# Weight sums of the last MLP: copies moved into the mixer's output stage, additions at four chosen tiles of the first tail

## Chip, cores and metric

The kernel runs on one core of a Trainium2 chip. The metric is the device time of one execution in microseconds (us). Five engines work from their own instruction queues: TensorE (PE in the profile), VectorE (DVE), ScalarE (ACT), GpSimd (POOL) and SyncE (SP), which issues most DMA transfers. The core has 16 DMA engines. Transfers that SP and ScalarE issue go through hardware queues (q1 in the profile), transfers that POOL issues through the software queue q0.

## What is computed

The reference is a transformer-like block followed by a second block of two layers, on 512 tokens of width 1024, in float32:

```
x = first_block(x, ...)        # attention + pooling + SSM mixer, w_out, top-2 of 16 experts
for i in range(2):             # second_block
    h = x * (1 + scale) + shift
    y = mla_mixer(h, ...) if i == 0 else s5_mixer(h, ...)
    x = layer_norm(ALPHA * x + (1 + gate) * y)
    h = x * (1 + scale) + shift
    y = relu(h @ w1[i] + b1[i]) ** 2 @ w2[i] + b2[i]
    x = layer_norm(ALPHA * x + (1 + gate) * y)
```

The change concerns the weights `w2[1]` (4096 x 1024), the down projection of the last MLP. The kernel multiplies it in 2 x 2 blocks in a scheme that needs seven block products in place of eight; four of them use sums of weight blocks. With 00, 01, 10 and 11 for the blocks (row block, column half), the sums are two = 00 + 01, right = 01 + 11, three = 00 + 01 + 11 and four = 00 + 01 + 11 + 10. Each is 4 MB. They depend on inputs alone, and are formed in DRAM by DMA transfers that POOL issues, long before they are read.

## The kernel before

The kernel is a list of stages, each an `nc.Block()` with one instruction stream for each engine. At a block's end every engine drains and meets a barrier of all engines, then the next stage begins (`Kernel.stage`). Within a stage engines meet through semaphores. A semaphore of a DMA transfer rises by 16 when the data have landed. Every float32 product is made of three products of rounded parts: ScalarE writes the high part of a weight tile (`high`), VectorE the low part (`low`), TensorE multiplies.

**The first place, `residual_stage` "mix_out" (L2162).** It is the product of the merged mixer with `w_out`, with residual and the sums of a layer norm. TensorE runs four weight tiles of 256 columns, all of whose weights are there by 980 us. POOL runs `router.widen` (L2293), which waits for two small router loads, and nothing after it. SP stores `mod_rows` (L2182) and loads the router weights. Then come `routing_stage` (L2405) and `experts_stage`. In routing, SP first issues two broadcasts `both_b` of 512 KB (L2443), a small row pair and six loads of 1 MB of the first expert's weights (L2348). VectorE uses `both_b` in `y_scaled` (L2626), for which TensorE's transposes wait. POOL makes constants (L2456 on) and later scatters the token rows by indirect DMA (L2477), which go through q0; SP waits for the scatters before it loads the next expert's tokens.

**The second place, `tail_stage` "tail0" (L3649).** It is the output product of the first mixer of the second block and the whole first MLP. Its loop runs over weight tiles n = 0 to 33 of 256 columns. A tile is 2 x 24 matmuls of 512 columns; `tile_done` rises by one for each of its two halves, so `tile_done` >= 12 means that n = 5 is through. SP loads tile n when `low(n - 3)` is done (L3722), 1 MB each. In the gaps VectorE forms parameters of the later S5 mixer (`beside(n)`): `input_powers` for n = 12 to 19 writes one room in SBUF, which SP stores to DRAM (`beside.store`, L4623) after the load of n = 18, 19, ... (`STORE_AT`). The next `input_powers` waits until that store has landed (L4723). VectorE's order in one round n is `square`, `low(n + 2)`, `hidden_low` or `add`, then `beside(n)`.

POOL ends `tail0` with `later.form` (L3755): eight DMA passes of 4 MB, four plain (`bypass`) and four accumulating (`add`), each issued when `tile_done` has reached 12, 18, 24, ... 54 and the pass before has landed (L3628 to L3632). The order is: 00 to two, + 01, two to three, + 11, 01 to right, + 11, three to four, + 10. The closing stage loads the sums at L4131, from 2332 us on.

Of the kernel before, what the change touches and what calls it, by code (L numbers as in the profile page):

```python
# [9 lines left out]
ALU = mybir.AluOpType  # L10
# [11 lines left out]
HT = HALF // P  # L22
# [2139 lines left out]
def residual_stage(k, name, halves, x, x_parts, alpha, gate, mod_rows, first, router):  # L2162

    ps = k.ps  # L2170
    base, N = halves.first[name], D // HALF
    norm_sems = [f"norm_{x}" for x in TokenNorm.SEMS]
    with k.stage(name, "x_high", "x_low", "x_scaled", "seventh_done", "evicted", "rows_stored", "router_loaded", "wide_ready", *norm_sems) as (block, s, sb):
        sq, sums = sb("sq", [P, 2, T]), sb("sums", [P, 2, T])
        norm = TokenNorm(k, s, "norm", 0, sq, sums[:, 0, :], sums[:, 1, :])
        rstd = ps[:, 3, :]

        @block.sync
        def _(sp):
            k.clear(sp)  # L2180
            for j in range(3):
                sp.dma_start(mod_rows[j:j + 1, :].rearrange("o (c p) -> p (o c)", p=P), k.mod[:, first + j * KD:first + (j + 1) * KD],  # L2182
                             allow_slow_non_contiguous=True).then_inc(s["rows_stored"], 16)
            router.load(sp, s["router_loaded"])
            sp.wait_ge(s["rows_stored"], 48)

        @block.gpsimd
        def _(pool):
            router.widen(pool, first, s["router_loaded"], s["wide_ready"])

        @block.tensor
        def _(pe):
            for n in range(N):
                outs = [ps[:, n * HT + f, :] for f in range(HT)]
                if n < N - 1:
                    halves.products(pe, base + n, x_parts, outs, arriving=(s["x_low"], 0) if n == 0 else None)
                else:
                    halves.product(pe, base + n, 0, x_parts, outs[0], final=False).then_inc(s["seventh_done"], 1)
                    halves.product(pe, base + n, 1, x_parts, outs[1], final=True)
                if n == 1:  # L2200
                    norm.pe_shift(pe)
            norm.pe_sums(pe)
            k.fill(pe, ps[:, 4, 0:P], 18)

        @block.scalar
        def _(act):
            def scaled(first, last):
                for c in range(first, last):
                    act.activation(k.x[:, c, :], k.x[:, c, :], ACT.Copy, scale=alpha).then_inc(s["x_scaled"], 1)

            for kk in range(KD):
                act.activation(x_parts[:, 0, kk], x[:, kk, :], ACT.Copy).then_inc(s["x_high"], 1)
            halves.high(act, base + 1)
            act.preload_act_table_set("natural_log_exp_and_others")
            scaled(0, 4)
            halves.high(act, base + 2)
            scaled(4, KD)
            halves.high(act, base + 3)
            for c in range(KD):
                norm.act_square(act, c)  # L2220
            norm.act_spread(act)
            act.wait_ge(norm.s["var_ready"], 1)
            act.activation(norm.rstd, norm.rstd, ACT.Ln, bias=k.eps_ln[:]).then_inc(norm.s["log_done"], 1)
            act.wait_ge(norm.s["log_done"], 1)
            act.activation(rstd, norm.rstd, ACT.Exp, scale=-0.5).then_inc(norm.s["root_done"], 1)

        @block.vector
        def _(dve):
            step = Steps(dve, s["evicted"])
            for kk in range(KD):  # L2230
                dve.wait_ge(s["x_high"], kk + 1)
                dve.tensor_tensor(x_parts[:, 1, kk], x[:, kk, :], x_parts[:, 0, kk].bitcast(F32), ALU.subtract).then_inc(s["x_low"], 1)
            halves.low(dve, base + 1)
            for n in range(N):
                if n + 2 < N:
                    halves.low(dve, base + n + 2)
                for c in range(n * HT, (n + 1) * HT):
                    if c == KD - 2:
                        dve.wait_ge(s["seventh_done"], 1)
                    else:  # L2240
                        dve.wait_ge(halves.half_used, base + n + 1)
                    dve.wait_ge(s["x_scaled"], c + 1)
                    step(dve.scalar_tensor_tensor(out=k.x[:, c, :], in0=ps[:, c, :], scalar=k.mod[:, gate + c:gate + c + 1], in1=k.x[:, c, :],
                                                  op0=ALU.mult, op1=ALU.add))
                    if c >= KD - 2:
                        norm.dve_shift(dve, c)
                if n < N - 1:
                    norm.dve_pair(dve, n)
            norm.dve_centre(dve, 0)
            norm.dve_centre(dve, 1)  # L2250
            norm.dve_var(dve)
            norm.dve_centre(dve, 2)
            norm.dve_centre(dve, 3)
# [1353 lines left out]
class WeightSums:  # L3607


    def __init__(self, k, name, w):  # L3610
        self.blocks = w.rearrange("(s two p) n -> two s p n", two=2, p=P)
        self.formed = k.stack.enter_context(k.nc.semaphore("sums_formed"))
        self.room = k.nc.dram_tensor(name, (K2 // 2, P, 4, STRIP), F32, kind="Internal").ap()

    def total(self, n):
# [3 lines left out]
    def block(self, odd, half):  # L3619
        return self.blocks[odd][:, :, half * STRIP:(half + 1) * STRIP]  # L3620

    def form(self, pool, products, every):

        two, three, right, four = (self.total(n) for n in range(4))
        n = 0
        for dst, first, then in ((two, self.block(0, 0), self.block(0, 1)), (three, two, self.block(1, 1)),
                                 (right, self.block(0, 1), self.block(1, 1)), (four, three, self.block(1, 0))):
            for src, op in ((first, ALU.bypass), (then, ALU.add)):  # L3628
                pool.wait_ge(products, every * (n + 2))
                pool.dma_start(dst, src, accum_op=op).then_inc(self.formed, 16)  # L3630
                n += 1
                pool.wait_ge(self.formed, 16 * n)  # L3632

    def source(self, i, q):

# [13 lines left out]
def tail_stage(k, layer, w_mix, x_parts, big, divided, ahead, beside, later):  # L3649
# [19 lines left out]
    with k.stage(name, "high_done", "low_done", "tile_done", "cols_step", "x_scaled", "evicted", "h_done", "x_high", "x_low", "x_ready",  # L3669
                 "relu_done", "squared", "hidden_high", "hidden_low", "added", "next_high", "next_low",  # L3670
                 *norm_sems, *S5Parameters.SEMS) as (block, s, sb):
        parts = divided
# [62 lines left out]
        def _(pool):  # L3735
# [16 lines left out]
            step(pool.tensor_scalar(vec[:, O_SCALE], g2, ALPHA_2, None, ALU.mult))  # L3752
            step(pool.tensor_scalar(vec[:, O_SHIFT], sh2, ALPHA_2, None, ALU.mult))
            pool.wait_ge(s["x_low"], KD)
            later.form(pool, s["tile_done"], 3 * HT)  # L3755

        @block.tensor
        def _(pe):
# [1618 lines left out]
def second_block(k, out, loads):  # L5377

    big, k.big_plain = shared(k, "big", [P, 2, K2 // 2, T])
    k.hp2, plain = shared(k, "h_parts_second", [P, 2, KD, T])  # L5380
    k.h, g = plain[:, 0], plain[:, 1]
    low_half, high_half = big[:, :, 0:KD, :], big[:, :, KD:, :]
    with ExitStack() as branch:
        sb = lambda n, shape: k.sb(n, shape, stack=branch)
        cq, ckv, k_pe = sb("cq", [P, QL // P, T]), sb("ckv", [P, T]), sb("k_pe", [ROPE, T])
        cos, sin = sb("cos", [ROPE, T]), sb("sin", [ROPE, T])
        latent_stage(k, loads, cq, ckv, k_pe, cos, sin)
        latent_attention_stage(k, cq, ckv, k_pe, cos, sin, low_half, k.ins["mla_w_o_2"][0])

    k.vec = k.sb("vec", [P, 9, KD])  # L5390
    parts, plain = shared(k, "late_parts", [P, 2, 2, KD, HALF])
    late = [plain[:, n].rearrange("p v k n -> p (v k n)") for n in range(2)]
    s5_input = S5Input(k, big)
    sums = WeightSums(k, "down_sums", k.ins["mlp_w2_2"][1])
    with ExitStack() as early:
        par = S5Parameters(k, lambda n, shape: k.sb(n, shape, stack=early))
        tail_stage(k, 0, k.ins["mla_w_o_2"][0], low_half, big, parts, s5_input, par, sums)
        u = late[0].rearrange("p (j g l c) -> p j g l c", j=S5_TILES, g=2, l=S5_HALF)
        both = 2 * S5_TILES * 2 * GC
        tab = S5Tables(k, late[1][:, both:])  # L5400
        resp = S5Responses(k, par, late[1][:, 0:both], lambda n, shape: k.sb(n, shape, stack=early))
        raw = late[1][:, 0:both].rearrange("p (k n) -> p k n", k=KD)
        s5_in_stage(k, u, s5_input, tab, resp)
        s5_stage(k, tab, par, resp, u, g, high_half, parts, raw)
    glu_stage(k, g, high_half, low_half, k.ins["ssm_w_out_2"][0], parts)
    closing_stage(k, 1, k.ins["ssm_w_out_2"][0], low_half, big, parts, sums, out)


def build(nc, ins, out):

    with ExitStack() as stack:
# [5 lines left out]
        with ExitStack() as strips:  # L5417
# [5 lines left out]
            k.mod_w = [flat[:, after + n * size:after + (n + 1) * size].rearrange("p (k n) -> p k n", k=KD // 2) for n in range(3)]  # L5423
            halves = Halves(k, stack)
            router = Router(k)
            mod_rows = nc.dram_tensor("mod_rows", (3, D), F32, kind="Internal").ap()
            with ExitStack() as mix:
                k.hp, plain = shared(k, "h_parts", [P, 2, KD, T], mix)
# [55 lines left out]
```

## Time and profile before

| | |
|---|---|
| time, median of 3 runs | 2647.94 us (2646.45 to 2650.1) |
| profiled execution, own time | 2652.91 us |
| its span | 2651.1 us, 33685 instructions |
| TensorE busy | 2476.3 us, 93% of the span |
| VectorE, ScalarE, POOL busy | 68%, 45%, 3% |
| DMA | 478.29 MB, mean 180 GB/s |
| software queue q0 | 22320 packets, 57.67 MB, 8.3% of 16 engines' span |

The profile gives for every instruction a start and a duration, the source line, the tiles written and read, and, where an engine was idle before it, what released it. A window view gives the busy time of each engine in a stretch, with the number of instructions that start in it, and the granted TensorE clock as a share of full speed. A DMA view gives for a stretch the packets and bytes of each queue, and for transfers issued in it the time from issue to landing.

### The profile page before, as it was taken

The numbers are of one execution on the slowest core, as the hardware profiler recorded it, in microseconds if no ns is written. First come the engines' busy times: TensorE is split into PE (matmuls) and PEld (weight loads), VectorE is DVE, ScalarE is ACT, GpSimd is POOL, SyncE is SP. The second block draws the span as 40 slices with busy tenths as digits, with TensorE's granted clock in tenths as the row PEclk, the third lists the DMA queues.
The fourth block names the chain that finished last, engine by engine and source line by source line (L and its number), as shares of the span: only waits on it lengthen the run. The fifth ranks groups of instructions, "written<-read, shape, count | busy, mean of one in ns | idle before, by whom it ended". The sixth has DMA issues, their size and how long they took to land. (4 is left out here: it accounts for less than half of the span.)

```text
span 2651.1 us, 33685 instructions
## 1 busy us (share of the span) xinstructions
PE 2476.3 (93%) x13175; PEld 1970.2 (74%) x13175; DVE 1789.7 (68%) x2553; ACT 1184.2 (45%) x1668; POOL 87.7 (3%) x184
## 2 busy tenths in 40 slices
PE   7999899999999999899988899998999989999996
PEld 5666678777777878788875457887888977788885
DVE  4899545587775666899965565675766574665557
ACT  5444422255564225588853343621324244365443
POOL 0000000000000000100001000000000000000001
PEclk9999999999999988999999999999999899999998
DMA  7887727333235744999962213598861414243446
GB/s 264 263 286 268 249 83 282 85 104 95 80 104 178 259 73 159 346 419 420 417 267 92 67 37 104 144 241 239 241 175 48 154 28 143 64 159 121 134 157 168
DMA packets 312398, 478.29 MB, mean 180 GB/s; under 512 B 29195, under 2 KB 198654, under 8 KB 302385
## 3 DMA queue, kind: packets, MB, share of 16 engines
q1 hardware_dynamic: 285392, 409.29, 45.4%
q0 software_dynamic: 22320, 57.67, 8.3%
q10 hardware_dynamic: 4528, 9.18, 0.9%
q8 instruction: 105, 1.72, 0.3%
q14 instruction: 53, 0.43, 0.1%
HBM read 431.82 MB, written 74.69 MB: 191 GB/s over the span
## 5 line engine op out<-in xcount | busy, mean ns | idle before, releaser
L2380 DVE TENSOR_TENSOR expert_parts<-w,expert_parts 128x2048 fp32r<-128x2048 f32 x102 | 232.6, 2288 | 21.2 <-ACT expert_parts L2376 20.8
L1345 PE MATMUL banks<-h_parts,ssm_parts 128*128 128x512 f32 x960 | 230.2, 397 | 0.8 <-DVE ssm_parts L1612 0.4
L3761 PE MATMUL banks<-big,late_parts 128*128 128x512 f32 x960 | 222.6, 394 | 5.7 <-DVE late_parts L3914 5.7
L2376 ACT ACTIVATE expert_parts<-w 128x2048 fp32r<-128x2048 f32 x102 | 194.7, 1916 | 60.2 <-PE banks L2387 51.8
L3761 PEld LDWEIGHTS banks<-big,late_parts 128*128 128x128 f32 x960 | 182.2, 190 | 45.2 <-issue 4.9
L1345 PEld LDWEIGHTS banks<-h_parts,ssm_parts 128*128 128x128 f32 x960 | 179.5, 189 | 43.7 <-issue 6.7
L2387 PE MATMUL banks<-expert_parts,expert_xt 128*128 128x512 f32 x816 | 192.1, 395 | 4.0 <-DVE expert_xt L2368 4.0
L2387 PEld LDWEIGHTS banks<-expert_parts,expert_xt 128*128 128x128 f32 x816 | 153.5, 190 | 36.4 <-DVE expert_xt L2368 4.7
L3761 PE MATMUL banks<-h_parts_second,late_parts 128*128 128x512 f32 x720 | 167.5, 393 | 7.5 <-DVE late_parts L3914 5.1
L3761 PEld LDWEIGHTS banks<-h_parts_second,late_parts 128*128 128x128 f32 x720 | 136.7, 190 | 36.6 <-issue 8.0
L4176 PE MATMUL banks<-h_parts_second,late_parts 128*128 128x512 f32 x512 | 159.4, 393 | 2.4 <-DVE h_parts_second L4406 2.4
L4194 PE MATMUL banks<-late_parts,big 128*128 128x512 f32 x448 | 137.9, 389 | 0.0
L882 PE MATMUL banks<-h_parts,front_parts 128*128 128x512 f32 x552 | 137.9, 400 | 0.0
L4396 DVE TENSOR_TENSOR w_parts<-w_second,late_parts 128x2048 fp32r<-128x2048 f32 x47 | 107.6, 2289 | 42.5 <-ACT late_parts L4282 42.2
L552 PE MATMUL banks<-h_parts,front_parts 128*128 128x512 f32 x576 | 132.3, 391 | 2.7 <-PEq L151 2.7
L552 PEld LDWEIGHTS banks<-h_parts,front_parts 128*128 128x128 f32 x576 | 108.0, 188 | 26.4 <-issue 4.2
L3823 ACT ACTIVATE late_parts<-w_second 128x2048 fp32r<-128x2048 f32 x35 | 66.9, 1914 | 135.2 <-PE banks L3761 135.2
L3914 DVE TENSOR_TENSOR late_parts<-w_second,late_parts 128x2048 fp32r<-128x2048 f32 x35 | 80.1, 2292 | 69.7 <-ACT late_parts L3823 68.9
L4282 ACT ACTIVATE late_parts<-w_second 128x2048 fp32r<-128x2048 f32 x47 | 89.7, 1912 | 82.2 <-DMA w_second<-in_mlp_w_dram 56.2
L552 PE MATMUL banks<-h_parts,ssm_parts 128*128 128x512 f32 x480 | 111.5, 394 | 5.9 <-DVE h_parts L1966 3.1
L882 PEld LDWEIGHTS banks<-h_parts,front_parts 128*128 128x128 f32 x552 | 101.7, 190 | 19.8
L1135 DVE SCALAR_TENSOR_TENSOR attention_mod_sum<-w,silu_c,attention_mod_sum 128x512 f32<-128x512 f32 x147 | 110.4, 751 | 4.7 <-DMA w<-in_mod_ffn_w_dram 0.3
(791 smaller groups left out, 4729.6 us busy)
## 6 DMA issues: line engine op xcount, KB each, us to landing
w_second<-in_mlp_w_dram SPq DMA_DIRECT2D x60, 1024.0 KB, 5.4
w<-in_w_exp_gate_dram SPq DMA_DIRECT2D x34, 1024.0 KB, 9.3
w<-in_w_exp_up_dram SPq DMA_DIRECT2D x34, 1024.0 KB, 9.0
w<-in_w_exp_down_dram SPq DMA_DIRECT2D x34, 1024.0 KB, 9.0
w<-in_w_in_dram SPq DMA_DIRECT2D x64, 512.0 KB, 4.6
w<-in_mod_mix_w_dram SPq DMA_DIRECT2D x24, 1024.0 KB, 5.1
down_sums<-in_mlp_w_dram POOLq DMA_DIRECT2D x6, 4096.0 KB, 31.3
w<-in_mod_ffn_w_dram SPq DMA_DIRECT2D x23, 1024.0 KB, 6.1
```

The costliest lines, as they stand in the source:

```text
L552: mm = pe.matmul(out, self.parts[:, n % 2, w, kk, f * P:(f + 1) * P], x[:, v, kk, :], start=(start and kk == 0 and j == 0), stop=(stop and ...
L882: mm = pe.matmul(ps[:, bank, :], parts[:, j, w, kk, :], k.hp[:, x, kk, :], start=(kk == 0 and n == 0), stop=(kk == KD - 1 and n == 2))
L1135: ins = dve.scalar_tensor_tensor(out=acc, in0=w, scalar=by, in1=acc, op0=ALU.mult, op1=ALU.add)
L1345: mm = pe.matmul(ps[:, t % 2, :], parts[:, t % SPLITS, w, kk, :], k.hp[:, x, kk, :], start=(kk == 0 and j == 0), stop=(kk == KD - 1 and j ...
L2376: act.activation(self.high_part(h), self.raw(h), ACT.Copy).then_inc(self.high_done, 1)
L2380: dve.tensor_tensor(self.low_part(h), self.raw(h), self.high_part(h).bitcast(F32), ALU.subtract).then_inc(self.low_done, 1)
L2387: mm = pe.matmul(out, x[:, v, first + kk, :], self.tile(h, w, kk), start=(start and kk == 0 and j == 0), stop=(stop and kk == KE - 1 and j ...
L3761: mm = pe.matmul(ps[:, bank(n, f), :], w_part(n, w)[:, kk, f * P:(f + 1) * P], x[:, v, kk, :], start=(first_chunk(n) and kk == 0 and j == ...
L4176: mm = pe.matmul(ps[:, bank(n, f), :], w_part(n, w)[:, kk, f * P:(f + 1) * P], x[:, v, kk, :], start=(kk == 0 and j == 0), stop=(kk == KD ...
L4194: mm = pe.matmul(ps[:, BANK[q] + j, :], hidden(STATIONARY[q], v)[:, kt, j * P:(j + 1) * P], strip_part(n, w)[:, kt, :], start=(kt == 0 and ...
L4282: act.activation(w_part(n, 0), raw_half(k, n), ACT.Copy).then_inc(s["high_done"], 1)
L4396: dve.tensor_tensor(w_part(n, 1), raw_half(k, n), w_part(n, 0).bitcast(F32), ALU.subtract).then_inc(s["low_done"], 1)
```

## The change

A new method `WeightSums.copy` starts four plain copies, of blocks 00, 00, 01 and 10, into the places of two, three, right and four. POOL calls it in stage `mix_out` after `widen`, and doesn't wait for the copies there. `form` in `tail0` keeps only accumulating passes, now four: two += 01 at `tile_done` 12, right += 11 at 20, three += right at 28, four += three at 54, each after the one before has landed. Before them POOL waits once for the copies (a new semaphore `sums_copied`). The object `k.sums` is made earlier in `build`, in place of in `second_block`.

```
@@ residual_stage
         def _(pool):
             router.widen(pool, first, s["router_loaded"], s["wide_ready"])
+            k.sums.copy(pool)
@@ class WeightSums
-    def form(self, pool, products, every):
+    def copy(self, pool):
+
+        for n, (odd, half) in enumerate(((0, 0), (0, 0), (0, 1), (1, 0))):
+            pool.dma_start(self.total(n), self.block(odd, half)).then_inc(self.copied, 16)
+
+    def form(self, pool, products):
 
         two, three, right, four = (self.total(n) for n in range(4))
-        n = 0
-        for dst, first, then in ((two, self.block(0, 0), self.block(0, 1)), (three, two, self.block(1, 1)),
-                                 (right, self.block(0, 1), self.block(1, 1)), (four, three, self.block(1, 0))):
-            for src, op in ((first, ALU.bypass), (then, ALU.add)):
-                pool.wait_ge(products, every * (n + 2))
-                pool.dma_start(dst, src, accum_op=op).then_inc(self.formed, 16)
-                n += 1
-                pool.wait_ge(self.formed, 16 * n)
+        pool.wait_ge(self.copied, 64)
+        for n, (dst, src, behind) in enumerate(((two, self.block(0, 1), 12), (right, self.block(1, 1), 20), (three, right, 28), (four, three, 54))):
+            pool.wait_ge(products, behind)
+            pool.dma_start(dst, src, accum_op=ALU.add).then_inc(self.formed, 16)
+            pool.wait_ge(self.formed, 16 * (n + 1))
@@ tail_stage
             pool.wait_ge(s["x_low"], KD)
-            later.form(pool, s["tile_done"], 3 * HT)
+            later.form(pool, s["tile_done"])
```

## Rows read from the trace of the kernel before

**Rows 1.** The page, part 1: busy time of TensorE, instructions.
```profile
PE 2476.3 (93%) x13175; PEld 1970.2 (74%) x13175; DVE 1789.7 (68%) x2553; ACT 1184.2 (45%) x1668; POOL 87.7 (3%) x184
```

**Rows 2.** Windows: stretch, length, busy (instructions) of five engines, clock, DMA share, GB/s.
```profile
980.00:1000.00 20.00, 20.00 (x88) 16.19 (x87) 12.99 (x18) 4.99 (x7) 0.14 (x1) 1.00 0.00 1
...
1020.00:1030.00 10.00, 8.53 (x47) 8.11 (x48) 4.06 (x9) 9.17 (x18) 0.00 (x0) 0.63 1.02 412
```

**Rows 3.** In order of time: start, duration, engine, line; end of mix_out, routing.
```profile
979.02 1.12 POOL L2301 TENSOR_TENSOR router_wide<-router_wide,mod 128x128 f32<-128x128 f32 x2 [21.04 <-DMA router_b<-in_b_router_dram]
...
1014.05 0.60 ACT L2225 ACTIVATE banks<-mix_out_sums 128x512 f32<-128x512 f32 x1
...
1015.85 0.10 POOL L2456 MEMSET routing_pair<- 128x4 f32 x1 [35.70 <-POOLq L151]
...
1024.14 0.69 DVE L2626 TENSOR_TENSOR expert_parts_plain<-expert_parts_plain,routing_both_b 128x512 f32<-128x512 f32 x1 [0.73 <-ACT expert_parts_plain L2564]
...
1055.44 1.17 POOL L2477 DMA_INDIRECT expert_rows<-expert_parts_plain,slots  x1 [38.24 <-DVE slots L2714]
```

**Rows 4.** DMA issues of the span: count, KB each, median us to landing.
```profile
down_sums<-in_mlp_w_dram POOLq DMA_DIRECT2D x6, 4096.0 KB, 31.3
...
down_sums<-down_sums POOLq DMA_DIRECT2D x2, 4096.0 KB, 20.2
...
routing_both_b<-mod_rows SPq DMA_DIRECT2D x2, 512.0 KB, 5.3
```

**Rows 5.** DMA queue, 1684 to 1694 us, first plain pass: packets, MB, share.
```profile
q0 software_dynamic: 745, 3.05, 100.9%
```

**Rows 6.** DMA queues, 409 to 411, then 423 to 425 us, POOL's zeroing.
```profile
q0 software_dynamic: 206, 0.84, 102.4%
...
q0 software_dynamic: 164, 0.67, 81.5%
q1 hardware_dynamic: 161, 0.16, 23.1%
```

**Rows 7.** In order of time, VectorE in tail0: the waits for a store.
```profile
1806.84 0.42 DVE L4856 TENSOR_TENSOR s_room<-s_held,s_b 128x256 f32<-128x256 f32 x1 [11.54 <-DMA s_inputs<-s_room]
...
1835.33 0.43 DVE L4856 TENSOR_TENSOR s_room<-s_held,s_b 128x256 f32<-128x256 f32 x1 [10.60 <-DMA s_inputs<-s_room]
```

**Rows 8.** In order of time, TensorE in tail0: its gaps.
```profile
1814.91 23.39 PE L3761 MATMUL banks<-big,late_parts 128*128 128x512 f32 x96 [3.51 <-DVE late_parts L3914]
1843.40 89.74 PE L3761 MATMUL banks<-h_parts_second,late_parts 128*128 128x512 f32 x384 [5.10 <-DVE late_parts L3914]
```

**Rows 9.** In order of time, POOL in tail0: four of eight passes.
```profile
1681.55 1.14 POOL L3630 DMA_DIRECT2D down_sums<-in_mlp_w_dram  x1 [82.03 <-PE banks L3761]
...
1779.34 1.85 POOL L3630 DMA_DIRECT2D down_sums<-in_mlp_w_dram  x1 [31.59 <-PE banks L3761]
1812.89 1.04 POOL L3630 DMA_DIRECT2D down_sums<-in_mlp_w_dram  x1 [31.70 <-DMA down_sums<-in_mlp_w_dram]
...
1922.97 1.83 POOL L3630 DMA_DIRECT2D down_sums<-in_mlp_w_dram  x1 [31.52 <-PE banks L3761]
```

**Rows 10.** In order of time, SP's DMA issues in tail0.
```profile
1772.25 0.37 SPq L3722 DMA_DIRECT2D w_second<-in_mlp_w_dram  x1
1779.02 0.37 SPq L4623 DMA_DIRECT2D s_inputs<-s_room  x1
1783.13 0.37 SPq L3722 DMA_DIRECT2D w_second<-in_mlp_w_dram  x1
1788.58 0.37 SPq L4623 DMA_DIRECT2D s_inputs<-s_room  x1
```

**Rows 11.** DMA issues, 1785 to 1790 us: us to landing.
```profile
s_inputs<-s_room SPq DMA_DIRECT2D x1, 512.0 KB, 18.2
```

**Rows 12.** Windows, TensorE alone: stretch, length, busy (matmuls), clock, DMA share, GB/s.
```profile
1820.00:1825.00 5.00, 5.00 (x24) 1.00 0.95 297
...
1843.40:1848.00 4.60, 4.60 (x11) 0.50 0.75 226
```

More of the change, by code:

```diff
@@ L3611, in __init__ @@
         self.blocks = w.rearrange("(s two p) n -> two s p n", two=2, p=P)
-        self.formed = k.stack.enter_context(k.nc.semaphore("sums_formed"))
+        self.copied, self.formed = (k.stack.enter_context(k.nc.semaphore(x)) for x in ("sums_copied", "sums_formed"))
         self.room = k.nc.dram_tensor(name, (K2 // 2, P, 4, STRIP), F32, kind="Internal").ap()
@@ L5393, in second_block @@
     s5_input = S5Input(k, big)
-    sums = WeightSums(k, "down_sums", k.ins["mlp_w2_2"][1])
     with ExitStack() as early:
         par = S5Parameters(k, lambda n, shape: k.sb(n, shape, stack=early))
-        tail_stage(k, 0, k.ins["mla_w_o_2"][0], low_half, big, parts, s5_input, par, sums)
+        tail_stage(k, 0, k.ins["mla_w_o_2"][0], low_half, big, parts, s5_input, par, k.sums)
         u = late[0].rearrange("p (j g l c) -> p j g l c", j=S5_TILES, g=2, l=S5_HALF)
@@ L5405, in second_block @@
     glu_stage(k, g, high_half, low_half, k.ins["ssm_w_out_2"][0], parts)
-    closing_stage(k, 1, k.ins["ssm_w_out_2"][0], low_half, big, parts, sums, out)
+    closing_stage(k, 1, k.ins["ssm_w_out_2"][0], low_half, big, parts, k.sums, out)
 def build(nc, ins, out):
@@ L5425, in build @@
             router = Router(k)
+            k.sums = WeightSums(k, "down_sums", k.ins["mlp_w2_2"][1])
             mod_rows = nc.dram_tensor("mod_rows", (3, D), F32, kind="Internal").ap()
```

## Prediction, made before the changed kernel was run

> **What bounds the kernel now.** I read the page first. TensorE is busy for 93% of the span [rows 1], so a microsecond counts only if TensorE loses or gains it, or if all engines wait together. The change touches two places; the windows, the order in time and the DMA view of both decide. The first place is the end of stage `mix_out`, where the copies go. TensorE runs there without a gap at a granted clock of 1.00, and the DMA engines move nothing from 980 to 1000 [rows 2]. POOL finishes `widen` at 980.1, ScalarE's last work of the stage ends at 1014.65, and routing starts on POOL at 1015.85 [rows 3]. The second place is `tail0`, where the eight passes run now. There the reader should look for DMA transfers that make a compute engine wait. VectorE waits twice for a store of S5 parameters, 11.54 and 10.60 us [rows 7], and each wait is followed by a gap on TensorE, 3.51 and 5.10 us [rows 8].
>
> **What the stores wait for.** `input_powers` may write its room again only when the store before it has landed. The store issued at 1788.58 came 9.2 us after the addition of 1779.34 [rows 9, 10] and took 18.2 us to land [rows 11]. That store blocked VectorE until 1806.8. The next load of MLP weights was queued on SP, but VectorE's order is what starves TensorE: its `low` of the coming tile stands behind `input_powers`. The second wait falls inside the plain copy of 1812.89.
>
> **Removed from the tail: four plain passes.** Additions stay at product tiles 12, 20, 28 and 54, one at a time. Tiles 12 and 30 are at 1681.55 and 1779.34 [rows 9], so a tile takes 97.8 / 18 = 5.43 us, and the four additions start at 1681.6, 1725.0, 1768.5 and again 1923.0. From row 4 an accumulating or mixed pass takes about 31 us, which the wait for `formed` hides. So the third addition ends near 1801, and none runs between there and 1923. The second stall then has no cause: **gain 5.10 us**. Its granted clock comes back too. In the 4.6 us after that gap the clock was 0.50 and 11 matmuls started, against 24 in an undisturbed 5 us [rows 12]. At 10.86 / 48 = 0.226 us each, 20 fit there, so 9 x 0.226 = **2.1 us** more. Together 7.2 us.
>
> The first stall I keep. The third addition now starts 10.9 us, exactly one weight tile, earlier. The load of 1772.25 is then 3.8 us into it and the store of 1779.02 is 10.6 us into it [rows 10], as the load of 1783.1 and the store of 1788.58 are now (3.8 and 9.2 us). Everything moves one weight tile forward: the store lands 27.4 us into the addition, at 1795.9, TensorE runs out at 1800.5 in place of 1811.4, and the gap is 3.5 us again. Bounds for this term: 0 (both stalls shift away, 5 us more gain) and 3 us worse, if the store waits for the whole 31 us. I take no change, since the phases agree to 1.4 us. Nothing else in the tail waits for these passes, and the closing stage first reads them 400 us later.
>
> **Added: four copies on POOL in `mix_out`.** POOL has nothing else there, each issue costs it 1 to 2 us [rows 9], and SP's and ScalarE's queues get nothing new. The data are 4 x 4 MB. Alone on the engines, the software queue q0 moved 745 packets in 10 us [rows 5]; one copy is 1,040 packets (4.19 MB of 4 KB). Four are 4,160 packets, 4,160 / 74.5 = 55.8 us. Issue at 980.5, packets 2.5 us later (the pass issued at 1681.55 filled the engines by 1684), plus some 0.5 us to land: **the copies end at 1039.3**. The stage's other engines end at 1014.65. Idle DMA time hides 34 us; about 25 us sticks out.
>
> What does that cost? **Here lies the choice.** A stage is one `nc.Block()`, and at its end each engine, POOL too, drains and meets a barrier. In the kernel before, every stage in which POOL starts a DMA either makes POOL wait for it or ends long after it has landed, so no row shows POOL crossing a stage's end with a transfer under way. Bound from below: POOL crosses freely, 0 at the barrier. Bound from above: POOL's drain holds until the last byte, and all five engines wait for it, 1039.3 - 1014.65 = 24.6 us. I take the upper one. q0 is the software queue: POOL itself is busy 1 to 2 us with each issue [rows 9], so the transfers are partly its own work, and the drain is the point at which an engine's work is to be empty. I am not sure of it, and both ends stay in the range. Queued behind POOL's drain are routing's constants, and everybody else's first instruction of routing.
>
> With the hold, TensorE idles some 25 us. Up to the stage's end the granted clock was 1.00, and from 1020 to 1030, where TensorE was busy 8.5 us of 10, it was down to 0.63 [rows 2]. After 25 idle us I take it to be at the lower level (1.2 GHz) from routing's start. The matmuls of 1016 to 1020 on the chain then take twice as long, about 1.5 us more (0 to 3).
>
> The Trainium skill speaks against my choice: "Perfetto Trace Analysis", section "DMA Instruction — SWDGE (GPSIMD)", says that such an instruction is over for POOL when the last descriptor is written, not when the data have moved. The row agrees for the instruction (1.1 to 1.9 us each, while its pass takes 19 to 33), but says nothing on a drain. By that rule read widely the sum would be that of rival 1.
>
> **Sum** against the profiled run: 2652.91 us (its span 2651.1 and 1.8 around it) + 24.6 + 1.5 - 7.2 = 2671.8. The median of the runs lies 5.0 us below the profiled one, so **2667 us**.
>
> **Rivals.**
> 1. *POOL passes the barrier; the copies run on into routing* (ends not slower). At 1018 some 1,550 packets are left. SP's two broadcasts `routing_both_b` at 1017.05 then share the engines. Where q0 and q1 both have work they go packet for packet, 164 to 161 [rows 6]. The broadcasts are 256 packets of 4 KB, 16 rounds, each with a copy packet of 16 / 74.5 = 0.215 us: 3.4 us, and some 2 us for a later first packet. They landed 5.3 us after issue [rows 4], and VectorE used them at 1024.14 [rows 3], 1.8 us of slack; TensorE's transposes wait for that. Loss 3.4 + 2 - 1.8 = 3.6 us. The copies would be through near 1058, just ahead of the scatter that shares their queue (1055.44 + 3.6). Net 3.6 - 7.2 = -3.6: **2644 us**, range 2637 to 2652. It decides wholly at the barrier: if routing starts at 1016, this is the case. Against it stands the drain; for it, that ScalarE and SP leave DMAs open across stages (SP's expert loads).
> 2. *Held, but the copies run at the best rate seen*, the zeroing's 206 packets in 2 us [rows 6]: 40.4 us, end 1023.9, hold 9.3, net +3.6: **2652 us**. Against it: that traffic writes from SBUF; DRAM to DRAM showed 74.5 per us. The Trainium skill's "DMA: Bandwidth & Descriptors", section "Anatomy of one DMA", gives 2.0 us plus bytes at 436 GB/s, about 40.5 us for 16.8 MB as an estimate, the same outcome; rows 5 (305 GB/s) disagree with it for this kind of copy.
> 3. *Held, and each copy costs what its pass in the tail did*, 20.2 us [rows 4]: 80.8 us, end 1062, hold 47, net +41: **2689 us**. Against it: those 20 us include MLP loads that shared the engines.
> 4. *The second stall stays* (the spacing doesn't do what it says), because stores late in the third addition back up: 7.2 us dearer, 2674 with the hold, 2652 without. The free stretch from 1801 to 1923 speaks against it.
>
> **How the numbers follow.** Forecast (held, near 305 GB/s) 0.60, its own range 2657 to 2677; rival 1 0.26; rival 2 0.06; rival 3 0.04; rival 4 0.04. The 8 in 10 range goes from 2642 to 2680; it leaves out the lower part of rival 1 and rival 3. A change of 0.2%, 5.3 us, is about what a measurement of this kernel can tell from none. Slower: forecast and rivals 3 and 4, and a little of 1, 0.69. Same: half of rival 1 and rival 2, 0.19. Faster: 0.12.
>
> **What would show it.** Held: the first instructions of routing at about 1040, POOL's among them, all engines idle from 1015 to then, q0 busy until just before. Passed: routing at 1016, `L2626` on VectorE later than 1024, q0 mixed with q1 until some 1058. Copy price: q0's packets in the windows from 983. Tail: one wait of VectorE for `s_inputs` near 1796 (plus the shift) and one gap on TensorE of 3 to 4 us, no second one; a stretch without q0 between the third and the fourth addition. I am wrong if routing starts on time, if the copies end before 1025, or if both gaps remain.

## The result: 1.0% slower, and the profile after

The changed kernel takes 2675.96 us (median) against 2649.02 us for the kernel before on the same chip, a ratio of 1.0103 with a 95% interval of 1.0076 to 1.013. The forecast was 2667 us, its range 2642 to 2680. The profiled execution took 2683.1 us, its span is 2681.3.

The windows of the changed kernel at the end of `mix_out` answer to [rows 2]. The columns are the same:

```profile
980.00:1000.00 20.00, 20.00 (x88) 16.20 (x87) 12.38 (x17) 4.30 (x5) 4.97 (x6) 1.00 0.80 237
1000.00:1020.00 20.00, 17.41 (x85) 12.95 (x83) 10.11 (x16) 4.41 (x7) 0.00 (x0) 1.00 0.99 281
1020.00:1030.00 10.00, 0.00 (x0) 0.00 (x0) 0.00 (x0) 0.00 (x0) 0.00 (x0) 0.53 0.98 275
1030.00:1040.00 10.00, 0.00 (x0) 0.00 (x0) 0.00 (x0) 0.00 (x0) 0.00 (x0) 0.50 1.03 290
1040.00:1044.00 4.00, 0.00 (x0) 0.00 (x0) 0.00 (x0) 0.00 (x0) 0.00 (x0) 0.50 0.55 194
```

From 1020 to 1044 no engine starts a single instruction, while the DMA engines are full until some 2 us before the end of it. In [rows 2] the same stretch, 1020 to 1030, held 47 matmuls. In order of time, the changed kernel (answers to [rows 3]):

```profile
981.39 0.90 POOL L2302 TENSOR_TENSOR router_wide<-router_wide,mod 128x128 f32<-128x128 f32 x2 [21.33 <-DMA router_b<-in_b_router_dram]
982.23 4.21 POOL L3626 DMA_DIRECT2D down_sums<-in_mlp_w_dram  x4
...
1015.88 0.60 ACT L2226 ACTIVATE banks<-mix_out_sums 128x512 f32<-128x512 f32 x1
...
1044.59 0.10 POOL L2457 MEMSET routing_pair<- 128x4 f32 x1 [58.14 <-POOLq L151]
1044.62 2.05 PE L158 MATMUL banks<-ident 128*128 128x128 f32 x8 [27.20 <-PEq L151]
...
1087.40 1.16 POOL L2478 DMA_INDIRECT expert_rows<-expert_parts_plain,slots  x1 [41.46 <-DVE slots L2715]
```

Read it so: POOL needs 4.21 us to issue the four copies and does nothing more in the stage. ScalarE's last work ends at 1016.5. The first instructions of routing, on POOL and on TensorE, stand at 1044.6, behind the stage's end (`L151`), not behind a semaphore of the stage. Before, `widen` and routing's first POOL instruction lay 1015.85 - 979.02 = 36.8 us apart [rows 3]; now 1044.59 - 981.39 = 63.2 us. **The hold is 26.4 us.**

The tail's rows answer to [rows 7], [rows 8] and [rows 9]: the four additions on POOL, a store's issue on SP, VectorE's wait for it, and TensorE's one gap (with the matmuls ahead of it).

```profile
1716.55 2.02 POOL L3634 DMA_DIRECT2D down_sums<-in_mlp_w_dram  x1 [82.06 <-PE banks L3764]
1760.00 1.89 POOL L3634 DMA_DIRECT2D down_sums<-in_mlp_w_dram  x1 [41.43 <-PE banks L3764]
1803.47 1.83 POOL L3634 DMA_DIRECT2D down_sums<-down_sums  x1 [41.58 <-PE banks L3764]
1951.44 1.80 POOL L3634 DMA_DIRECT2D down_sums<-down_sums  x1 [146.14 <-PE banks L3764]
...
1814.06 0.37 SPq L4626 DMA_DIRECT2D s_inputs<-s_room  x1
...
1832.31 0.42 DVE L4859 TENSOR_TENSOR s_room<-s_held,s_b 128x256 f32<-128x256 f32 x1 [14.16 <-DMA s_inputs<-s_room]
...
1799.82 35.75 PE L3764 MATMUL banks<-big,late_parts 128*128 128x512 f32 x157
1840.37 9.80 PE L3764 MATMUL banks<-big,late_parts 128*128 128x512 f32 x36 [4.80 <-DVE late_parts L3917]
```

One gap on TensorE (4.80 us) is left of two. From the addition behind tile 12 to that behind tile 54 it is 1951.44 - 1716.55 = 234.9 us; before, 1922.97 - 1681.55 = 241.4 [rows 9]. **The tail gives 6.5 us.**

The span is 30.2 us longer, and it adds up from one first instruction of POOL to the next: up to `widen` +2.4 (ahead of the change; the kernels below have `widen` between 976.6 and 982.5 where nothing ahead of it was changed), hold +26.4, routing +3.2 (42.8 us to its first scatter against 39.6), the experts +1.6, latent stages +1.4, tail -6.5, the rest +1.7. The experts and the latent stages differ by as much between kernels in which nothing there was changed (338.7 to 340.4 us and 199.0 to 200.9 us in the runs below), so those 3.0 us are not put down to the change. The profiled execution is also the slowest of the four. What the change itself does is 26.4 + 3.2 - 6.5 = **+23.1 us**.

### The profile page after: what moved, and what is told of

Read it like the earlier page. It is cut to its first block and busy times, and to the rows that moved or that the text cites. A ratio compares the mean times of both kernels' runs of the same rounds, so it can differ in the third digit from the quotient of the medians.

```text
span 2681.3 us, 33682 instructions
## 1 busy us (share of the span) xinstructions
PE 2481.2 (93%) x13175; PEld 1974.8 (74%) x13175; DVE 1789.4 (67%) x2553; ACT 1184.1 (44%) x1668; POOL 87.4 (3%) x184
## 5 line engine op out<-in xcount | busy, mean ns | idle before, releaser
L2381 DVE TENSOR_TENSOR expert_parts<-w,expert_parts 128x2048 fp32r<-128x2048 f32 x102 | 232.6, 2288 | 23.1 <-ACT expert_parts L2377 22.3
L2388 PEld LDWEIGHTS banks<-expert_parts,expert_xt 128*128 128x128 f32 x816 | 152.9, 189 | 36.5 <-DVE expert_xt L2369 4.8
L3764 PEld LDWEIGHTS banks<-h_parts_second,late_parts 128*128 128x128 f32 x720 | 135.1, 188 | 30.5 <-issue 2.5
L4399 DVE TENSOR_TENSOR w_parts<-w_second,late_parts 128x2048 fp32r<-128x2048 f32 x47 | 107.6, 2289 | 41.6 <-ACT late_parts L4285 41.5
L4285 ACT ACTIVATE late_parts<-w_second 128x2048 fp32r<-128x2048 f32 x47 | 89.7, 1912 | 81.9 <-DMA w_second<-in_mlp_w_dram 56.1
```

The costliest lines, as they stand in the source:

```text
L2381: dve.tensor_tensor(self.low_part(h), self.raw(h), self.high_part(h).bitcast(F32), ALU.subtract).then_inc(self.low_done, 1)
L2388: mm = pe.matmul(out, x[:, v, first + kk, :], self.tile(h, w, kk), start=(start and kk == 0 and j == 0), stop=(stop and kk == KE - 1 and j ...
L3764: mm = pe.matmul(ps[:, bank(n, f), :], w_part(n, w)[:, kk, f * P:(f + 1) * P], x[:, v, kk, :], start=(first_chunk(n) and kk == 0 and j == ...
L4285: act.activation(w_part(n, 0), raw_half(k, n), ACT.Copy).then_inc(s["high_done"], 1)
L4399: dve.tensor_tensor(w_part(n, 1), raw_half(k, n), w_part(n, 0).bitcast(F32), ALU.subtract).then_inc(s["low_done"], 1)
```

## Experiments

The theory: POOL's drain at the end of `mix_out` waits for the copies, and all wait for POOL; nothing else in the change costs much. The rival: the stage's end is held or lengthened by something else that goes with the copies (traffic on the engines, the price of any DMA in flight). All ratios are against the kernel before on the same chip.

### The drain taken away, then a wait put in its place

First kernel: `mix_out` is a block whose POOL doesn't drain at its end. The added wait is for `widen`'s four small writes, not for the copies.

```diff
-            with self.nc.Block() as block:
+            with self.nc.Block(no_gpsimd_drain=no_drain) as block:    # True for mix_out alone
...
             router.widen(pool, first, s["router_loaded"], s["wide_ready"])
+            pool.wait_ge(s["wide_ready"], 4)
             k.sums.copy(pool)
```

> The changed kernel, with one difference: at the end of stage mix_out POOL meets the barrier without draining first (it waits for its own four small writes in its place). Theory D, POOL's drain waits for the copies: routing's first POOL instruction comes at its old distance from widen, 37 us behind it and not 63, while q0 still moves copies; the time falls by about 26 us less what the copies cost inside routing (my rival 1: 3.6 us), so 20 to 23 us under the changed kernel, and 3 to 4 us under the kernel before (ratio to before about 0.999). Theory S, saturated DMA engines hold the stage's end by themselves (instruction fetch, semaphores of other transfers): routing still starts some 26 us late, and the ratio to before stays at 1.010.

Measured: 2650.12 us, ratio 0.9997 (0.9986 to 1.0008). POOL in order of time, without the drain:

```profile
982.51 0.90 POOL L2303 TENSOR_TENSOR router_wide<-router_wide,mod 128x128 f32<-128x128 f32 x2 [21.58 <-DMA router_b<-in_b_router_dram]
983.71 4.21 POOL L3627 DMA_DIRECT2D down_sums<-in_mlp_w_dram  x4 [0.30 <-POOL router_wide L2303]
1018.64 0.10 POOL L2458 MEMSET routing_pair<- 128x4 f32 x1 [30.72 <-POOLq L151]
...
1063.89 1.17 POOL L2479 DMA_INDIRECT expert_rows<-expert_parts_plain,slots  x1 [43.90 <-DVE slots L2716]
```

Routing starts 36.1 us after `widen`, as before: the hold is gone with the drain. In exchange routing takes 45.2 us, 5.7 longer, since the copies now run beside its loads (they are through near 1055). The waits in routing (us in total, times, longest), then its DMA issues, show where:

```profile
DVE expert_parts_plain L2628 <- DMA routing_both_b<-mod_rows: 6.5, 1, 6.5
```

```profile
routing_both_b<-mod_rows SPq DMA_DIRECT2D x2, 512.0 KB, 11.4
```

The broadcasts land after 11.4 us in place of 5.3 [rows 4], VectorE waits 6.5 us, TensorE's transposes with it. VectorE's first use of them comes 14.1 us behind routing's start against 8.3, which is the whole of the 5.7. In this kernel's profile the tail takes 236.1 us from tile 12 to 54, a gain of 5.4 us, so what is lost and what is gained cancel. Over the nine kernels here that have four additions with the third at tile 28, the tail's gain is 5.3 to 6.5 us. This is rival 1 of the prediction, built.

Second kernel: still no drain, but POOL waits for its copies' semaphore before it leaves the stage.

```diff
             k.sums.copy(pool)
+            pool.wait_ge(k.sums.copied, 64)
```

> The kernel without POOL's drain in the residual stage, with an explicit wait of POOL for its four copies at that stage's end in the drain's place. Theory (the drain holds because it waits for the copies' last descriptor, and nothing else of it costs): the hold is back whole, routing starts 60 to 63 us after the widening against 36.1 without the wait, and the time is the changed kernel's, 2674 to 2677 us. Rival (the drain costs of itself, or the stage's end is held by something else that the missing drain also removed): routing starts earlier than 55 us after the widening and the time stays under 2665 us.

Measured: 2674.91 us, ratio 1.0102 (1.0081 to 1.0122).

```profile
979.39 1.18 POOL L2304 TENSOR_TENSOR router_wide<-router_wide,mod 128x128 f32<-128x128 f32 x2 [20.86 <-DMA router_b<-in_b_router_dram]
...
1042.48 0.10 POOL L2459 MEMSET routing_pair<- 128x4 f32 x1 [57.40 <-POOLq L151]
```

63.1 us from `widen` to routing against 63.2 in the changed kernel. A plain wait for the copies' landing costs the same as the drain did. So the drain waits until the copies have landed. The kernel with fillers below keeps the drain and shows 61.7 us, so a price of the drain itself of up to 1.5 us could not be told from the noise of these three profiles.

### Two and three copies in the stage

Some copies go to the start of the SSM stage, 480 us earlier. `copy` takes the numbers of the sums that it starts.

```diff
# SSM stage, POOL, behind its memsets
+            k.sums.copy(pool, (2, 3))     # second kernel: (3,)
# mix_out
-            k.sums.copy(pool)
+            k.sums.copy(pool, (0, 1))     # second kernel: (0, 1, 2)
```

> The changed kernel with two of the four copies in mix_out and the other two at the start of ssm. Theory D: two copies are 2080 packets, 28 us at 72 to 75 per us, so they land near 1013 (widen's end + 31 us), before ScalarE's last instruction of the stage: no hold, routing starts 37 us after widen, and the ratio to before is that of e2, 0.997 to 0.999. If crossing the stage's end costs something for any POOL transfer issued in it, whether landed or not, routing starts later than that.

> Three copies beside the output product, the fourth in the SSM stage. Theory (the hold is the copies' end less the stage's own end): three copies take about 42 us from 1 us behind the widening, so routing starts 45 to 48 us after it, a hold of 9 to 13 us; the one copy in the SSM stage costs 5 to 8 us (two cost 13); with the tail's 6.5 us back the time is 2658 to 2665 us. Rival (the hold is a fixed price that any copy still in flight at the drain brings): routing starts 60 us after the widening, and the time is over 2672 us.

Measured: two and two 2654.38 us, ratio 1.0017 (1.0006 to 1.0027); three and one 2661.1 us, ratio 1.0042 (1.0027 to 1.0056). POOL in the first, then in the second:

```profile
993.00 0.90 POOL L2303 TENSOR_TENSOR router_wide<-router_wide,mod 128x128 f32<-128x128 f32 x2 [22.40 <-DMA router_b<-in_b_router_dram]
...
1028.13 0.10 POOL L2458 MEMSET routing_pair<- 128x4 f32 x1 [32.17 <-POOLq L151]
```

```profile
979.92 0.89 POOL L2303 TENSOR_TENSOR router_wide<-router_wide,mod 128x128 f32<-128x128 f32 x2 [22.22 <-DMA router_b<-in_b_router_dram]
...
1027.56 0.10 POOL L2458 MEMSET routing_pair<- 128x4 f32 x1 [43.67 <-POOLq L151]
```

From `widen` to routing: 35.1 us with two copies (no hold), 47.6 with three, 63.2 with four. The fourth adds 15.6 us, that is 4.19 MB / 15.6 us = 269 GB/s. The hold is no fixed price; it is what of the copies sticks out behind the stage's own end. The first kernel was expected under the time of the kernel before and is above it: the SSM stage was not free, as the next kernel shows.

### All four copies in the SSM stage

```diff
# SSM stage, POOL, behind its memsets
+            k.sums.copy(pool)
# mix_out
-            k.sums.copy(pool)
```

> The changed kernel with all four copies issued by POOL at the start of stage ssm, 450 us before mix_out ends, where the DMA engines move 80 to 100 GB/s and POOL has nothing until 591 us. The additions in the first tail are those of the changed kernel. Theory D: no hold anywhere, mix_out ends on time; what is left is the tail's gain of 6.5 us, less what loads in ssm lose to 55 us of copies (0 to 4 us): ratio to before 0.997 to 0.999. A rival, that the other 4 us of loss which the profile shows (in glu, in experts) come from the changed additions or the new place of the sums in DRAM: then the ratio is 1.000 or above. If copies cost time wherever they are, by HBM traffic, it is above 1.001.

Measured: 2673.69 us, ratio 1.0096 (1.0079 to 1.0113), as slow as the change. There is no hold (`widen` 1002.91, routing 1039.39: 36.5 us), but `widen` itself comes 23.9 us later. Of this kernel, a row of the waits from 495 to 620 us, then the DMA queues from 510 to 535 us, when both had work all the time, and the input weights' issues from 495 to 560 us; the last fence is the issues' row of the kernel before, 495 to 560 us:

```profile
ACT ssm_parts L1479 <- DMA w<-in_w_in_dram: 45.1, 5, 16.6
```

```profile
q0 software_dynamic: 1817, 7.32, 86.0%
q1 hardware_dynamic: 1816, 0.92, 14.3%
...
w<-in_w_in_dram SPq DMA_DIRECT2D x6, 512.0 KB, 30.5
```

```profile
w<-in_w_in_dram SPq DMA_DIRECT2D x11, 512.0 KB, 3.8
```

SP's queue q1 and the copies' queue q0 went packet for packet, 1816 to 1817. But a packet of the copies carries 4 KB (7.32 MB / 1817) and one of SP's 0.5 KB, so the loads got a seventh of the engines' busy time (14.3 to 86.0%), and a 512 KB load that landed in 3.8 us took 30.5 (medians). ScalarE waited 45.1 us for these loads, in the kernel before not at all. One window shows what it cost TensorE, busy 8.49 us of 20 where it had been busy for all of them; this kernel, then the kernel before:

```profile
520.00:540.00 20.00, 8.49 (x37) 6.37 (x35) 5.11 (x10) 2.06 (x3) 0.00 (x0) 0.86 1.00 322
```

```profile
520.00:540.00 20.00, 20.00 (x96) 16.41 (x95) 17.17 (x25) 7.09 (x10) 0.00 (x0) 1.00 0.45 124
```

The first square of that stage is POOL's `ssm_sq`, in this kernel and in the kernel before:

```profile
617.84 1.30 POOL L1332 TENSOR_TENSOR ssm_sq<-ssm_sq 128x512 f32<-128x512 f32 x1 [114.82 <-ACT ssm_sq L1547]
```

```profile
591.31 1.29 POOL L1331 TENSOR_TENSOR ssm_sq<-ssm_sq 128x512 f32<-128x512 f32 x1 [92.54 <-ACT ssm_sq L1546]
```

From POOL's first instruction of the stage (498.22 and 498.13) it is 119.6 us against 93.2, 26.4 us more. With two copies there it is 106.0 us, 12.8 more; with one 94.8, 1.6 more, where 5 to 8 had been expected. (Kernels with no copy there show 93.2 to 94.8, so one copy's price is not shown to be other than nothing.) ScalarE's waits for the input weights go the same way: 45.1 us with four copies, 19.0 with two, 4.6 with one. The weights go into four buffers by turns (`L1210`); that these catch a short burst and not a long one is how I read it, no run changes their number. I had expected this place to be free: a DMA share under 0.6 says nothing of how small the transfers are that live in it.

The Trainium skill says, in "DMA: Bandwidth & Descriptors", section "Queues, rings and completion order", that each DMA engine goes round its queues at packet granularity. The counts of the two queues, 1816 to 1817, agree.

### TensorE kept busy into the hold

105 more filler matmuls behind the output product, so that the clock doesn't fall before routing.

```diff
-            k.fill(pe, ps[:, 4, 0:P], 18)
+            k.fill(pe, ps[:, 4, 0:P], 18 + 105)
```

> The changed kernel, with 105 more filling products (128 columns, results unused) on TensorE at the end of mix_out, in the 25 us in which it would wait for the barrier. Their results are used by nobody. If the 3.2 us that routing takes longer after the hold are the lower clock, the granted clock at routing's start is 1.00 again, the stretch from routing's first instruction to the first scatter shrinks from 42.8 to 39.6 us, and the time is about 3 us under the changed kernel's. If they are something else (DMA traffic, a late load), routing stays 42.8 us long, and the time doesn't change.

Measured: 2673.87 us, ratio 1.0091 (1.0074 to 1.0108). Windows of this kernel before and behind routing's start (1040.4), then of the changed one (start 1044.6), then of the kernel with the explicit wait (start 1042.5):

```profile
1035.00:1040.00 5.00, 3.86 (x35) 3.67 (x33) 0.00 (x0) 0.00 (x0) 0.00 (x0) 1.00 0.59 209
1040.00:1045.00 5.00, 4.59 (x32) 4.52 (x32) 4.55 (x10) 1.91 (x3) 1.28 (x10) 0.78 0.46 135
1045.00:1050.00 5.00, 4.72 (x24) 4.41 (x22) 2.95 (x6) 3.43 (x7) 0.00 (x0) 0.50 1.01 406
```

```profile
1044.00:1049.00 5.00, 4.38 (x21) 4.41 (x21) 4.35 (x9) 1.70 (x3) 1.29 (x10) 0.50 0.38 125
1049.00:1054.00 5.00, 5.00 (x26) 5.00 (x26) 3.13 (x6) 2.26 (x3) 0.00 (x0) 0.50 1.01 397
```

```profile
1047.00:1052.00 5.00, 5.00 (x34) 5.00 (x34) 3.03 (x6) 2.77 (x5) 0.00 (x0) 0.69 1.03 397
```

The clock was 1.00 up to routing and fell soon behind it all the same; routing took 41.5 us against 42.8. But the kernel with the explicit wait, without any filler, took 41.1 (1042.48 to 1083.58). So the fillers are not shown to bring anything, and the times' intervals overlap. The clock falls in the kernel before too, without a hold: 0.96 from 1018 to 1023 and 0.50 in the next 5 us.

What is left is a loss in routing after a hold. The seven kernels here with neither a hold nor copies running on into routing take 39.6 or 39.7 us for it; the four with a hold take 41.1 (explicit wait), 41.2 (three copies), 41.5 (fillers) and 42.8 (the change). That is 1.5 to 3.2 us. In the slowest of the four the clock stands at 0.50 in every window from 1044 to 1074, with the explicit wait it is 0.69 and 0.65 in two of them. That fits the colder clock as the cause; no run isolates it.

### The copies in the latent attention, and the third addition later

POOL is idle there for 130 us and the DMA share is 0.31 at first, then 0.18 and 0.09. The copies wait for the first head's query product.

```diff
# latent attention stage
+        @block.gpsimd
+        def _(pool):
+            pool.wait_ge(s["qn_done"], 1)
+            k.sums.copy(pool)
```

The second kernel has, beside this, the third addition behind tile 42 in place of 28:

```diff
-... (three, right, 28), (four, three, 54)
+... (three, right, 42), (four, three, 54)
```

> The four copies go to the latent attention stage, where the trace of the kernel before has the DMA engines busy 9 to 23% and POOL idle from 1428 to 1594; they wait there for the first head's query product. Theory (the change loses only by the place of its copies: POOL's drain in the residual stage, loads held up in the SSM stage): routing starts 35 to 37 us after the widening, as before, no stage is longer, and the second tail stall stays gone: 6.5 us under the kernel before, ratio 0.997 to 0.998, near 2644 us. Rival (the copies cost wherever they run, since loads of the attention's heads queue behind 4 KB packets as the input weights did in the SSM stage): the heads' 192 KB loads go from 2.5 us to over 14 us, a head's length, PE waits for them, the latent attention is 5 to 15 us longer, ratio 1.000 to 1.003.

> As the kernel with the copies in the latent attention stage, and the third addition at tile 42 in place of 28, behind the last of the eight S5 parameter stores. Theory (the stall that is left in the tail, 4.8 us of PE and the colder clock behind it, comes from a store that runs in the shadow of the third addition): that gap goes too, 5 to 7 us less than the other kernel, near 2638 us, ratio 0.995. Rival (the additions slow whatever small transfer they meet, and at tile 42 they meet the next ones): a gap of like size elsewhere between tiles 42 and 54, or the fourth addition now late, and the time is that of the other kernel within 0.1%.

Measured: tile 28 2652.09 us, ratio 1.0004 (0.9995 to 1.0012); tile 42 2646.8 us, ratio 0.9977 (0.9968 to 0.9986). The rival won for the place: of the first kernel, from 1425 to 1600, a row of the waits and one of the DMA issues:

```profile
PEld banks L3299 <- DMA latent_attention_wkv<-in_mla_w_kvb_dram: 16.1, 2, 8.7
```

```profile
latent_attention_wkv<-in_mla_w_kvb_dram SPq DMA_DIRECT2D x8, 128.0 KB, 8.2
```

A head's 128 KB load takes 8.2 us (median of eight) against 2.6 before. That is less than the rival told for the heads' loads, but TensorE waits twice, 16.1 us in all, and from the combine's first gather to the tail's first POOL instruction it is 209.6 us against 199.6. This eats the tail's gain. The theory held for the tail: with tile 42 the last of the eight stores of `s_inputs` is issued (1848.19) just ahead of the third addition (1848.47), and tiles 12 to 54 take 228.5 us against 234.9 with tile 28. The stall that the change left is worth 6.5 us too.

### Copies only where nothing small runs

Two copies stay in `mix_out`, where two fit. The other two follow the frequencies' memsets in the latent stage, which issues no load but its positions.

```diff
# mix_out
+            k.sums.copy(pool, (0, 1))
# latent stage, POOL, behind its 64 memsets
+            k.sums.copy(pool, (2, 3))
```

> The same places for the copies, with the third addition at tile 28 as in the changed kernel. Theory: what the change was to bring and nothing else, one tail stall of two gone: 6.5 us under the kernel before, ratio 0.997 to 0.998, near 2645 us, and a gap of near 5 us left between tiles 28 and 40. Rival (the hold in the latent stage): 2650 to 2658 us, and the difference to the kernel with tile 42 is still 6.5 us.

> Two copies stay beside the output product, where two cost nothing (routing starts 35 us after the widening); the other two go to POOL's end of the latent stage, from about 1430 us, where the trace of the kernel before shows a DMA share of 0.00 until its attention's loads are issued at 1466.65; the third addition goes behind tile 42. Theory (a copy costs only what it holds up: a drain when it is the last to end, or small loads when it runs beside them): two copies at 14 us each end near 1459, before both, so no stage is longer, and the tail's two stalls, 6.5 us each with the clock behind them, are gone: 13 us under the kernel before, ratio 0.995 to 0.996, near 2639 us. Rival (the latent stage ends sooner than the copies, and its drain holds them as the other did): the heads' first loads are issued 5 to 15 us later and the time is 2644 to 2652 us.

Measured: tile 28 2646.15 us, ratio 0.9984 (0.9974 to 0.9993); **tile 42 2635.17 us, ratio 0.9946 (0.9933 to 0.9959)**, faster than both kernels. Of the latter, POOL and SP in order of time, then its windows of the latent stage:

```profile
1425.97 2.44 POOL L3629 DMA_DIRECT2D down_sums<-in_mlp_w_dram  x2 [0.28 <-issue]
...
1464.19 0.39 SPq L3283 DMA_DIRECT2D latent_attention_wq<-in_mla_w_qb_dram  x1
```

```profile
1425.00:1440.00 15.00, 13.88 (x27) 5.76 (x28) 8.94 (x16) 1.88 (x2) 3.13 (x27) 0.83 0.81 243
1440.00:1455.00 15.00, 15.00 (x36) 5.47 (x35) 9.39 (x17) 4.34 (x6) 0.00 (x0) 1.00 1.02 277
1455.00:1464.00 9.00, 5.13 (x12) 1.80 (x10) 1.21 (x2) 1.91 (x3) 0.00 (x0) 1.00 0.17 68
```

The copies are through near 1457, and SP's first issue of the next stage stands at 1464.2. Combine to tail is 200.0 us against 199.6, `widen` to routing 36.4 us. The tail with tile 28, then TensorE with tile 42 over the same tiles and beyond:

```profile
1802.61 12.75 PE L3767 MATMUL banks<-big,late_parts 128*128 128x512 f32 x49 [4.81 <-DVE late_parts L3920]
```

```profile
1744.11 87.20 PE L3767 MATMUL banks<-big,late_parts 128*128 128x512 f32 x384
1831.15 81.08 PE L3767 MATMUL banks<-h_parts_second,late_parts 128*128 128x512 f32 x357
```

With tile 42 TensorE runs from 1744 to 1912 without a gap. Tiles 12 to 54 take 228.5 us, 13.0 less than before; the medians lie 15.7 apart, and the interval of the ratio reaches from 11 to 18 us. The two kernels of this section lie 11.0 us apart where the trace has 6.5 for the stall between them; their profiled executions, with spans of 2633.3 and 2637.0 us, lie 3.7 apart. So what one stall is worth in the time stays open within a few us; in the tail itself it is 6.5.

## Why the prediction was right, step by step

1. **The choice: the drain holds.** Right, and shown: taken away, the hold goes; replaced by a wait for the landing, it comes back whole; with fewer copies it shrinks to nothing. The prediction had only a reason for it, that the transfers are partly POOL's own work, and said so. The runs show that the drain waits, not why, so the reason is still a guess that came out. The Trainium skill's rule from "Perfetto Trace Analysis", section "DMA Instruction — SWDGE (GPSIMD)", holds for the instruction (four in 4.21 us of POOL) and doesn't reach to the drain behind it.
2. **The hold's size, 24.6 us forecast, 26.4 measured.** The end of the copies was put at 1039.3, on `widen`'s 980.1. `widen` came 2.4 us later, which moves both ends. The rate was a little lower than in [rows 5]: the windows show 275 and 290 GB/s where [rows 5] gave 305. Rivals 2 and 3, with their other rates, are out. The Trainium skill's figure of 436 GB/s ("DMA: Bandwidth & Descriptors", section "Anatomy of one DMA — SWDGE (gpsimd) path"), weighed in rival 2, would have ended them in some 40 us, an estimate; here they take near 60.
3. **The colder clock, 1.5 us forecast, 3.2 measured in routing (1.5 with the explicit wait).** The clock is as told: granted at 0.50 from the first matmul. That all of the 3.2 us comes from it is not shown. In the kernel before, windows of 5 us from 1013 on show 1.00 and 0.96, so TensorE's first bank for ScalarE came 6.9 us after routing's start (1022.77, 1015.85), and in the changed kernel 9.8 us (1054.44, 1044.6). So 2.9 of the 3.2 us are lost before that bank is read. The forecast had doubled the matmuls of the first 4 us only.
4. **The second tail stall goes.** Right: one gap, one long wait. 7.2 us forecast, 6.5 measured. (The forecast's 9 x 0.226 is 2.0, not 2.1, which changes nothing.)
5. **The first stall stays.** Right, and closely: the store was to be issued 10.6 us into the third addition and was (1814.06 - 1803.47). TensorE was to run out at 1800.5 + 35.0 (the tail's shift) = 1835.5, and ran out at 1835.6. The store landed 1.4 us later than forecast, and the gap is 4.8 us where 3.5 were told. The forecast's own numbers had this: a store that is issued 10.6 us into the addition and takes 18.2 us again, as it did, lands 28.8 us into it, and the forecast kept the old 27.4. That is why the tail's gain is a little under 7.2.
6. **What rival 1 would give.** Its price in routing was put at 3.6 us; without the drain it measured 5.7. The late broadcasts were the right place. They landed 6.1 us later (medians, 11.4 against 5.3), not 5.4, and the clock fell to 0.53 in the wait (window 1028 to 1033 of that kernel). It came to 2650.1 against 2651.2 for the kernel before on that chip, 1.1 us less and not 3.6, and lies inside the range told for it.

The sum of the steps was +18.9 us, their measured sum +23.1. Most of what is missing is in the hold (1.8) and in routing (1.7). The medians differ by 26.9, with an interval from 20 to 34; the kernel with the explicit wait, which has the same hold, differs by 23.2. So no further term is needed, and none is ruled out below the width of that interval.

The prediction also had why the change fails, in its own sum: the place has 34 us of idle DMA time, and the data want 56. What it did not draw from it is the remedy. Two of the four copies need 28 us by the same rate and fit: with two in this place the way from `widen` to routing is 35.1, 36.4 and 36.8 us in three kernels, against 36.8 with none.

## What to carry to other kernels

- A prefetch or copy on GpSimd's queue belongs to the stage in which it is issued, up to its landing: here a stage whose end has GpSimd's drain did not end before it. Count bytes over the measured rate (here some 280 GB/s from DRAM to DRAM) against the time that is left in the stage, and split what doesn't fit.
- A low DMA share isn't free room. Ask how large the packets and how deep the buffers are that live there. A long transfer of 4 KB packets slowed loads of 0.5 KB packets eightfold (3.8 to 30.5 us). Two copies cost the SSM stage 12.8 us; the latent stage, whose DMA share had been 0.00, took two for nothing (200.0 us from combine to tail against 199.6).
- Space a large transfer away from small stores that somebody waits for. The stalls of this tail came from a store issued 8 to 11 us into a pass over DRAM, and the tail gained some 6.5 us with each that went (5.3 to 6.5 for the first).

## What the runs showed of the hardware

- POOL's drain at a block's end waits for the data of its outstanding transfers. From `widen` to routing it is 63.2 us with the drain, 36.1 without, 63.1 with a wait for the landing in its place.
- Copies from DRAM to DRAM ran at 275 to 290 GB/s on full engines (share 0.98 to 1.03), in packets of 4 KB.
- With packets of 4 KB on q0 and 0.5 KB on q1, both queues busy, the engines moved 1817 of the one and 1816 of the other in 25 us, and gave them 86.0% and 14.3% of their time.
- The price of copies beside small loads isn't proportional: one copy (4 MB) in the SSM stage cost 1.6 us at most, two 12.8, four 26.4.
- The fillers' effect on the clock was short: at 1.00 until routing's start, 0.78 in the 5 us across it, 0.50 in the next 5.
